# Ten of the 22 contraction tiles of the down projection as five pairs of seven half-block products

## The chip, the cores and the metric

One NeuronCore of a Trainium2 chip runs the whole program, and it is alone on the chip. The metric is the device time of one execution in microseconds (us). Lower is better. The kernel is written by hand, engine by engine: each engine has its own list of instructions, and semaphores are the only thing that orders one list against another. The engines are TensorE (PE; its weight loads are listed as PEld), VectorE (DVE), ScalarE (ACT), GpSimd (POOL) and SyncE (SP), which issues the DMAs.

## The reference

Two layers (DEPTH 2) run over x of 512 positions by 1024 channels, in float32. Each layer is a mixer (gMLP gating and differential attention) and a SwiGLU; the change is in the last product of the SwiGLU:

```python
for l in range(DEPTH):
    ...
    h = rms_norm(x, pre_ffn_g[l])
    gu = jnp.einsum('bsd,df->bsf', h, w_gate_up[l])
    gate, up = gu[..., :FFN_HIDDEN], gu[..., FFN_HIDDEN:]
    y = jnp.einsum('bsf,fd->bsd', jax.nn.silu(gate) * up, w_down[l])
    x = x + rms_norm(y, post_ffn_g[l])
```

FFN_HIDDEN is 2816, that is 22 contraction tiles of 128 (`FT`).

## The kernel before

**Three passes.** Every float32 factor is kept as a high part (a copy rounded to fp32r) and a low part (the factor less its high part, again fp32r). `product` (L594 to L597) issues three matmuls for each pair of tiles: high by high, low by high, high by low. So each weight block is copied by ACT to `w_hi` (`high`, L1060) and subtracted by POOL to `w_lo` (`low`, L529, two pieces of 128x512).

**Weights.** Weights come in chunks c = 0 to NC-1. A chunk has two halves h, each of 128x1024 floats (512 KB). `raw` holds two chunks, `w_hi` and `w_lo` two chunks as well, looked at as eight slots of 128x512 where the gate and up projections need it. SP's `load_half` (L439) reads a half once the lows of the same half two chunks before are made; `high` waits for the data and for the slot's earlier user (`w_done`, which PE raises).

**Gate and up.** Tiles f = 0 and 1 are plain. From f = 2 (`F0`) on, one chunk per f is a 2x2 block matrix B (rows: halves of the contraction; columns: gate and up), and the left factor is 2x2 as well (halves of the positions by halves of the contraction). They are multiplied with seven block products instead of eight (`gate_up_blocks`, L789), in the form with sums S1 to S4 of the left factor and T1 to T4 of B. DVE makes the T sums (`t_sum`, L1771), POOL five of seven lows, DVE two. T1 and T2 lie in PSUM banks, so that most of DVE's instructions there have one operand in PSUM.

**Down.** The hidden matrix (high `hid_hi`, low `hid_lo`, 128 x 22 x 512 each: contraction tile by positions) is the stationary factor, the weights stream as 512 columns. Eleven chunks of four tiles, first all 22 tiles of the left 512 output columns, then of the right ones. For each half chunk (two tiles) PE runs four rows of 128 positions, 6 matmuls each (`down_part`, L816), into banks 0 to 3 (left) and 4 to 7 (right). The last two chunks go row by row (`down_rows`, L825), so that the rows of the result end one after the other. Both `turn_rows` calls of the next group's first two rows (transposes of the normalised x) stand in the midst of rows 2 and 3.

```python
for c in range(C_DOWN, LAST - 1):
    for h in range(2):
        half, k = divmod(4 * (c - C_DOWN) + 2 * h, FT)
        rows = (2, 3, 0, 1) if k == 0 and half == 0 else (0, 1, 2, 3)
        for r in rows:
            ...
            down_part(l, c, h, r, rows[-1])
```

**Before the first down chunks.** SP has loaded the first two down chunks while the gate and up projections ran. When their last product is done, it issues four reads of 512 KB of x from the spill buffer, `gpost`, in layer 0 `gpre` (each of 1024 values for 128 partitions), and only then the third down chunk (L504 to L511).

**The boundary.** For each row of positions: ACT squares the right half (`root_of_branch`, L1108), DVE multiplies by the gain and adds to x (`residual`, L1534), ACT takes the root of the new row, DVE normalises it (`norm_row`, L1497), PE turns it. After layer 1 the same is done without the next norm, and the row is stored.

## Time and profile before

| | |
|---|---|
| median of 3 runs | 1084.99 us (1084.96 to 1085.32) |
| profiled execution | 1084.86 us |
| its span, first to last instruction | 1082.7 us |
| PE busy | 1074.8 us, 99% of the span |
| PEld, DVE, ACT, POOL busy | 89%, 56%, 54%, 52% |
| granted TensorE clock, mean | 0.999 |
| HBM traffic over the span | 109 GB/s |

The profiled execution is 2.2 us longer than its span; the rest lies ahead of the first instruction and behind the last one. Busy shares are of the span; a line number is that of the kernel before. Matmuls overlap in the records: the time from one start to the next, not the duration, is what one costs.

### The profile page before, as it was taken

How to read it: one execution, taken by the hardware profiler on the slowest of the kernel's cores; microseconds unless marked ns; L12 is line 12 of the kernel's file. 1: busy time of each engine (PE TensorE's matmuls, PEld its weight loads, DVE VectorE, ACT ScalarE, POOL GpSimd, SP SyncE). 2: the span in 40 equal slices, each digit the busy share in tenths (PEclk: the TensorE clock that was granted, in tenths of full speed). 3: DMA queues.
4: the chain of work that ended last, by engine and by line, in shares of the span. 5: the costliest groups of instructions: out<-in, count | busy, mean ns of one | idle time of the engine just before them, and what ended most of it. 6: DMA issues, size and time to landing. Idle time of an engine off the chain costs nothing.

```text
span 1082.7 us, 17501 instructions
## 1 busy us (share of the span) xinstructions
PE 1074.8 (99%) x6788; PEld 965.0 (89%) x6788; DVE 608.6 (56%) x1011; ACT 589.5 (54%) x1151; POOL 568.1 (52%) x442
## 2 busy tenths in 40 slices
PE   9999999999999999999999999999999999999997
PEld 7888788999999999888888888889999999988886
DVE  4376554878888884010344756457888888820103
ACT  6767784755555554221457568656655555531212
POOL 3534364467666665544344344634766666654440
PEclk9999999999999999999999999999999999999999
DMA  8423212424433434523353222232343343363212
GB/s 291 147 60 104 71 59 81 153 79 118 117 100 97 118 103 169 176 97 97 87 161 103 78 79 78 75 126 87 103 117 100 96 117 107 91 218 119 98 51 78
DMA packets 145335, 119.37 MB, mean 110 GB/s; under 512 B 3802, under 2 KB 120036, under 8 KB 145252
## 3 DMA queue, kind: packets, MB, share of 16 engines
q1 hardware_dynamic: 145236, 118.24, 35.1%
q8 instruction: 54, 0.88, 0.3%
q14 instruction: 29, 0.24, 0.1%
q10 hardware_dynamic: 16, 0.00, 0.0%
HBM read 111.94 MB, written 6.29 MB: 109 GB/s over the span
## 4 chain that ended last, share of the span: by engine, by line
PE 99%; ACT 0%; DMA 0%; DVE 0%; issue 0%; DVEq 0%; ACTq 0%
PE banks L595 30%; PE banks L597 30%; PE banks L596 30%; PE banks L660 2%; PE banks L688 2%; PE banks L604 1%; PE banks L673 1%; PE banks L865 1%; PE banks L699 1%; DMA x_rows<-in_x_dram 0%; PE banks L706 0%; ACT junk L1080 0%; PE banks L950 0%; DVE scratch L1509 0%; DVE x_rows L1543 0%
## 5 line engine op out<-in xcount | busy, mean ns | idle before, releaser
L534 POOL TENSOR_TENSOR w_lo<-raw,w_hi 128x512 fp32r<-128x512 f32 x204 | 264.7, 1321 | 312.2 <-ACT w_hi L1072 312.2
L552 POOL TENSOR_TENSOR w_lo<-raw,w_hi 128x512 fp32r<-128x512 f32 x200 | 260.8, 1314 | 146.6 <-ACT w_hi L1141 142.1
L595 PE MATMUL banks<-xg_hi,w_hi 128*128 128x256 f32 (+1 forms) x880 | 273.5, 311 | 0.0
L597 PE MATMUL banks<-xg_lo,w_hi 128*128 128x256 f32 (+1 forms) x880 | 271.3, 308 | 0.0
L596 PE MATMUL banks<-xg_hi,w_lo 128*128 128x256 f32 (+1 forms) x880 | 271.2, 308 | 0.0
L1072 ACT ACTIVATE w_hi<-raw 128x1024 fp32r<-128x1024 f32 x102 | 107.2, 1061 | 161.4 <-PE banks L597 146.9
L1141 ACT ACTIVATE w_hi<-raw 128x512 fp32r<-128x512 f32 x200 | 125.1, 630 | 114.9 <-DVE raw L1794 61.1
L597 PEld LDWEIGHTS banks<-xg_lo,w_hi 128*128 128x128 f32 x880 | 168.0, 191 | 8.4
L595 PEld LDWEIGHTS banks<-xg_hi,w_hi 128*128 128x128 f32 x880 | 168.1, 191 | 8.3
L596 PEld LDWEIGHTS banks<-xg_hi,w_lo 128*128 128x128 f32 x880 | 168.1, 191 | 7.5
L595 PE MATMUL banks<-w_hi,hid_hi 128*128 128x512 f32 x352 | 137.2, 390 | 0.0
L597 PE MATMUL banks<-w_lo,hid_hi 128*128 128x512 f32 x352 | 137.0, 389 | 0.0
L596 PE MATMUL banks<-w_hi,hid_lo 128*128 128x512 f32 x352 | 137.0, 389 | 0.0
L595 PE MATMUL banks<-s_part,w_hi 128*128 128x256 f32 x480 | 135.8, 283 | 0.0
L596 PE MATMUL banks<-s_part,w_lo 128*128 128x256 f32 x480 | 135.8, 283 | 0.0
L597 PE MATMUL banks<-s_part,w_hi 128*128 128x256 f32 x480 | 135.8, 283 | 0.0
L595 PEld LDWEIGHTS banks<-s_part,w_hi 128*128 128x128 f32 x480 | 92.2, 192 | 0.0
L596 PEld LDWEIGHTS banks<-s_part,w_lo 128*128 128x128 f32 x480 | 92.2, 192 | 0.0
L597 PEld LDWEIGHTS banks<-s_part,w_hi 128*128 128x128 f32 x480 | 92.2, 192 | 0.0
L1800 DVE TENSOR_TENSOR w_lo<-banks,w_hi 128x512 fp32r<-128x512 f32 x80 | 54.8, 686 | 51.8 <-ACT w_hi L1141 51.8
L1531 DVE TENSOR_TENSOR banks<-banks,gpost 128x512 f32<-128x512 f32 x16 | 10.6, 696 | 126.6 <-ACT junk L1106 126.6
L597 PEld LDWEIGHTS banks<-w_lo,hid_hi 128*128 128x128 f32 x352 | 66.1, 188 | 13.8
(180 smaller groups left out, 1875.8 us busy)
## 6 DMA issues: line engine op xcount, KB each, us to landing
raw<-in_w_gate_up_dram SPq DMA_DIRECT2D x88, 512.0 KB, 4.1
raw<-in_w_down_dram SPq DMA_DIRECT2D x44, 512.0 KB, 3.8
raw<-in_w_in_dram SPq DMA_DIRECT2D x40, 512.0 KB, 3.8
raw<-in_w_out_dram SPq DMA_DIRECT2D x16, 512.0 KB, 3.7
x_spill<-x_rows SPq DMA_DIRECT2D x8, 512.0 KB, 4.3
x_rows<-x_spill SPq DMA_DIRECT2D x8, 512.0 KB, 4.9
x_rows<-in_x_dram SPq DMA_DIRECT2D x4, 512.0 KB, 7.4
out_dram<-x_rows SPq DMA_DIRECT2D x8, 256.0 KB, 2.1
```

Of the source, the lines that this page charges most:

```text
L534: last = tt(lo[:, piece], raw_half(l, c, h)[:, piece], hi[:, piece].bitcast(F32), ALU.subtract)
L552: tt(lo, full, hi.bitcast(F32), ALU.subtract).then_inc(w_ready, 1)
L595: mm(o, stat[0], mov[0], start=first, stop=False)
L596: mm(o, stat[1], mov[0], start=False, stop=False)
L597: return mm(o, stat[0], mov[1], start=False, stop=last)
L604: last = tr(b_tr[turned_bank(group, r, half)][:, k, :], xn[:, r % 2, at:at + P], ident[:, :])
L660: last = mm(bank[SC_BANKS[n % 2][j]][:, 0:w], q[ps, h, i * P:(i + 1) * P], k[ps, h, 0:w], start=(n_pass == 0), stop=(n_pass == 2))
L673: last = tr(b_tr[T_BANK][:, at + k, :], attn[n % 2][:, k * P:(k + 1) * P], ident[:, :])
L688: last = mm(bank[O_BANK][:, (n % 2) * P:(n % 2 + 1) * P], attn_t(n, k), v_att[:, k, h * P:(h + 1) * P], start=(k == 0), stop=(k == i))
L1072: fn(high_low(l, c, h)[0], raw_half(l, c, h), ACT.Copy).then_inc(w_hi_ready, 1)
L1141: fn(factor(l, f, i)[0], full, ACT.Copy).then_inc(w_hi_ready, 1)
L1800: tt(lo, t_place(l, f, i), hi.bitcast(F32), ALU.subtract).then_inc(t_ready, 1)
```

## The change

The down projection takes tiles 0 to 9 as five pairs. In each pair the 2x2 left factor A has the first and the second tile of the pair as columns and positions 0 to 255 and 256 to 511 as rows; B has the two tiles as rows and the left and right 512 output columns as columns. Seven products stand for eight:

- chunk P (one per pair): A11 by B11 into banks 4 and 5, A12 by B21 into banks 0 and 1, S3 by T3 into 6 and 7, A22 by T4 into 2 and 3; each 2 row blocks by 3 passes, 24 matmuls for the chunk
- chunk Q (one per pair, read from HBM once more without B21): S4 by B22 into 4 and 5, S1 by T1 into 6 and 7, S2 by T2 into 0 and 1; 18 matmuls
- tiles 10 to 21 stay plain, 48 matmuls a chunk: `("L", 10)`, `("L", 14)`, `("L", 18)`, called left 10, left 14 and left 18 here, and right 10, right 14, right 18.

Over the five pairs the products accumulate in the banks, and DVE puts the results together afterwards: `add_p7`, `add_left`, `add_p6_left`, `add_p5`, `add_p6`. The left half of y now lies in SBUF (`y_left_of`). In the boundary each row of the right half gets one more addition on DVE ahead of ACT's square. Through the gate and up projections, copies and lows of f = 0 to 9 are cut in two or get a further addition.

All sums of the weights are DVE instructions with both inputs in `raw` or `w_hi`, in SBUF; `pair_sums` makes three for P and two for Q, `pair_lows` two for each. `h_sums` and `h_low` are four and four instructions of 128x1280, both inputs in SBUF.

```diff
     C_VG, C_QK, C_VA, C_QK2, C_U, C_OUT, C_GU = 0, 2, 4, 6, 8, 10, 14
     C_DOWN = C_GU + FT
-    NC = C_DOWN + 2 * FT // 4
+    NP = 5
+    K0_PLAIN = 2 * NP
+    DOWN = [("L", 10), ("P", 0), ("P", 1), ("L", 14), ("P", 2), ("P", 3), ("P", 4), ("L", 18),
+            ("Q", 0), ("Q", 1), ("Q", 2), ("Q", 3), ("Q", 4), ("R", 10), ("R", 14), ("R", 18)]
+    NC = C_DOWN + len(DOWN)
...
+    C_P, C_Q = [[C_DOWN + DOWN.index((kind, p)) for p in range(NP)] for kind in "PQ"]
+    C_L_END, C_R0 = C_DOWN + DOWN.index(("L", 18)), C_DOWN + DOWN.index(("R", 10))
+    P_B11, P_B21, P_T3, P_T4 = range(4)
+    Q_B22, Q_T1, Q_T2 = range(3)
...
+        H_PARTS = {"A11": (hid_hi[:, first_of_pair, left], hid_lo[:, first_of_pair, left]),
+                   "A12": (hid_hi[:, second_of_pair, left], hid_lo[:, second_of_pair, left]),
+                   "A22": (hid_hi[:, second_of_pair, right], hid_lo[:, second_of_pair, right]),
+                   "S3": (part_hi[:, 0:NP, :], hid_lo[:, first_of_pair, right]),
+                   "S1": (part_hi[:, NP:2 * NP, :], hid_hi[:, first_of_pair, right]),
+                   "S2": (part_hi[:, 2 * NP:3 * NP, :], part_lo[:, 0:NP, :]),
+                   "S4": (part_lo[:, NP:2 * NP, :], part_lo[:, 2 * NP:3 * NP, :])}
+        H_FULL = {"S3": hid_full[:, 1, first_of_pair, right], "S1": hid_full[:, 0, first_of_pair, right],
+                  "S2": part_full[:, 1, 0:NP, :], "S4": part_full[:, 1, 2 * NP:3 * NP, :]}
+        H_SUMS = ("S3", "S1", "S2", "S4")
...
+        def y_left_of(r):
+            return hid_full[:, r // 2, 4 + 2 * (r % 2):6 + 2 * (r % 2), left]
...
-                    sp.wait_ge(w_ready, low_upto(m, d, LOW_OF[B22 if h else T4] if blocks(d) else h))
+                    if kind_of(d) == "P":
+                        if h == 0:
+                            sp.wait_ge(w_ready, low_upto(m, d, P_B21))
+                            sp.wait_ge(pair_added, pair_added_upto(m, d, 2))
+                        else:
+                            sp.wait_ge(pair_ready, pair_upto(m, d, 1))
+                    elif kind_of(d) == "Q":
+                        if h == 1:
+                            sp.wait_ge(w_ready, low_upto(m, d, Q_B22))
+                        sp.wait_ge(pair_ready, pair_upto(m, d, 1))
+                    else:
...
+            def pair_low(l, c, i):
+                hi, lo = factor_of(l, c, i)
+                pool.wait_ge(w_hi_ready, upto(l, c, i))
+                tt(lo, pair_raw(l, c, i), hi.bitcast(F32), ALU.subtract).then_inc(w_ready, 1)
...
+                start = K0_PLAIN if kind == "L" or r >= 2 else None
+                last = wide_part(l, c, h, o, hid_left(r), range(k, k + 2), start, FT - 1)
                 if r == last_row:
                     last.then_inc(w_done, 1)
                 elif k + 2 == FT:
-                    last.then_inc(y_b_done if half else y_a_done, 1)
+                    last.then_inc(y_b_done if kind == "R" else y_a_done, 1)
...
+            def pair_product(l, c, i, part, o, first, last):
+                p = DOWN[c - C_DOWN][1]
+                hi, lo = factor_of(l, c, i)
+                for j in range(2):
+                    at = slice(j * P, (j + 1) * P)
+                    done = product(bank[o + j][:, :], (H_PARTS[part][0][:, p, at], H_PARTS[part][1][:, p, at]), (hi, lo),
+                                   first and p == 0, last and p == NP - 1)
+                done.then_inc(w_done, 1)
...
+            def left_pair(l, p):
+                c = C_P[p]
+                if p == 0:
+                    pe.wait_ge(hid_ready, FT * (l + 1))
+                pe.wait_ge(w_ready, low_upto(l, c, P_B11))
+                pair_product(l, c, P_B11, "A11", 4, True, True)
+                pe.wait_ge(w_ready, low_upto(l, c, P_B21))
+                pair_product(l, c, P_B21, "A12", 0, False, False)
+                pe.wait_ge(pair_ready, pair_upto(l, c, 0))
+                if p == 0:
+                    pe.wait_ge(h_ready, 4 * l + 1)
+                pair_product(l, c, P_T3, "S3", 6, True, True)
+                pe.wait_ge(pair_ready, pair_upto(l, c, 1))
+                pair_product(l, c, P_T4, "A22", 2, False, False)
...
+            def right_pair(l, p):
+                c = C_Q[p]
+                pe.wait_ge(w_ready, low_upto(l, c, Q_B22))
+                if p == 0:
+                    pe.wait_ge(h_ready, 4 * (l + 1))
+                    pe.wait_ge(p1_kept, 2 * (l + 1))
+                pair_product(l, c, Q_B22, "S4", 4, True, False)
+                pe.wait_ge(pair_ready, pair_upto(l, c, 0))
+                if p == 0:
+                    pe.wait_ge(p7_added, 2 * (l + 1))
+                pair_product(l, c, Q_T1, "S1", 6, True, True)
+                pe.wait_ge(pair_ready, pair_upto(l, c, 1))
+                if p == 0:
+                    pe.wait_ge(y_left_added, 4 * l + 2)
+                pair_product(l, c, Q_T2, "S2", 0, True, True)
...
                     gate_up_blocks(l, f)
                 for c in range(C_DOWN, LAST - 1):
-                    for h in range(2):
-                        half, k = divmod(4 * (c - C_DOWN) + 2 * h, FT)
-                        rows = (2, 3, 0, 1) if k == 0 and half == 0 else (0, 1, 2, 3)
-                        for r in rows:
-                            if c == C_DOWN and h == 0 and r < 2:
...
-                        act.wait_ge(w_done, upto(l - 1, C_DOWN + 6, 0))
+                        act.wait_ge(w_done, upto(l - 1, C_Q[1], Q_T1))
...
+                def pair_high(c, i):
+                    kind, p = DOWN[c - C_DOWN]
+                    if (kind, i) in (("P", P_B11), ("P", P_B21), ("Q", Q_B22)):
+                        n = NC * l + c
+                        act.wait_ge(raw_landed[n % 2][kind == "Q"], 16 * (n // 2 + 1))
+                    else:
+                        act.wait_ge(pair_added, pair_added_upto(l, c, {P_T3: 0, P_T4: 2}[i] if kind == "P" else i - 1))
+                    if ring[l, c, i][1] is not None:
+                        act.wait_ge(w_done, ring[l, c, i][1])
+                    fn(factor_of(l, c, i)[0], pair_raw(l, c, i), ACT.Copy).then_inc(w_hi_ready, 1)
...
+                    act.wait_ge(w_done, upto(l, C_P[NP - 1], P_B11))
+                    fn(silu_t[:, j, :], bank[4 + j][:, :], ACT.Copy).then_inc(p1_kept, 1)
...
                 silu_21(FT - 1)
                 hidden_high(FT - 1)
+                h_high("S3")
                 for c in range(C_DOWN + 1, NC):
-                    both_high(l, c)
-                    if c == C_DOWN + 6:
+                    if paired(c):
+                        for i in range(DONE_OF[kind_of(c)]):
+                            pair_high(c, i)
+                    else:
+                        both_high(l, c)
+                    if c == C_P[3]:
+                        for name in H_SUMS[1:]:
+                            h_high(name)
+                    elif c == C_L_END:
...
+                y_b = y_right_of(b, r)
+                if b % 2:
+                    if r < ST - 1:
+                        dve.wait_ge(y_b_done, 3 * b + r + 1)
+                    else:
+                        dve.wait_ge(w_done, upto(b // 2, LAST, 1))
+                    dve.wait_ge(p6_added, ST * (b // 2) + r + 1)
+                    tt(y_b, y_b, silu_t[:, r, :], ALU.add).then_inc(y_b_added, 1)
                 dve.wait_ge(ssq_b_ready, ST * b + r + 1)
...
+                def h_sums():
+                    a11, a12 = [[t.bitcast(F32) for t in H_PARTS[name]] for name in ("A11", "A12")]
+                    s1, s2, s4 = [H_FULL[name] for name in ("S1", "S2", "S4")]
+                    tt(s2, s1, a11[0], ALU.subtract).then_inc(h_added, 1)
+                    dve.wait_ge(h_added, 4 * l + 1)
+                    tt(s2, s2, a11[1], ALU.subtract).then_inc(h_added, 1)
+                    dve.wait_ge(h_added, 4 * l + 2)
+                    tt(s4, a12[0], s2, ALU.subtract).then_inc(h_added, 1)
+                    dve.wait_ge(h_added, 4 * l + 3)
+                    tt(s4, s4, a12[1], ALU.add).then_inc(h_added, 1)
...
+                def pair_sums(c):
+                    n = NC * l + c
+                    for h in range(2):
+                        dve.wait_ge(raw_landed[n % 2][h], 16 * (n // 2 + 1))
+                    b11, b12, b22 = [raw_half(l, c, col)[:, row * SE:(row + 1) * SE] for row, col in ((0, 0), (0, 1), (1, 1))]
+                    if kind_of(c) == "P":
+                        b21 = raw_half(l, c, 0)[:, SE:2 * SE]
+                        tt(b12, b22, b12, ALU.subtract).then_inc(pair_added, 1)
+                        dve.wait_ge(pair_added, pair_added_upto(l, c, 0))
+                        tt(b22, b12, b11, ALU.add).then_inc(pair_added, 1)
+                        dve.wait_ge(pair_added, pair_added_upto(l, c, 1))
+                        tt(b22, b21, b22, ALU.subtract).then_inc(pair_added, 1)
+                    else:
+                        tt(b12, b12, b11, ALU.subtract).then_inc(pair_added, 1)
+                        dve.wait_ge(pair_added, pair_added_upto(l, c, 0))
+                        tt(b11, b22, b12, ALU.subtract).then_inc(pair_added, 1)
...
+                def pair_lows(c):
+                    for i in (P_T3, P_T4) if kind_of(c) == "P" else (Q_T1, Q_T2):
+                        hi, lo = factor_of(l, c, i)
+                        dve.wait_ge(w_hi_ready, upto(l, c, i))
+                        tt(lo, pair_raw(l, c, i), hi.bitcast(F32), ALU.subtract).then_inc(pair_ready, 1)
...
+                def add_p6_left(j):
+                    y = y_left_of(2 + j)
+                    if j == 0:
+                        dve.wait_ge(w_done, upto(l, C_Q[NP - 1], Q_T2))
+                    dve.wait_ge(y_left_added, 4 * (l + 1))
+                    tt(y, y, in_two(bank[j][:, :]), ALU.add).then_inc(y_left_ready, 1)
...
+                    pair_lows(C_P[p])
+                    if p == 1:
+                        h_sums()
+                for name in H_SUMS[1:]:
+                    h_low(name)
+                add_p7(0)
+                add_p7(1)
+                pair_sums(C_Q[0])
+                pair_lows(C_Q[0])
+                pair_sums(C_Q[1])
+                for r in range(ST):
+                    add_left(r)
+                pair_lows(C_Q[1])
+                for p in range(2, NP):
+                    pair_sums(C_Q[p])
+                    pair_lows(C_Q[p])
+                add_p6_left(0)
+                add_p6_left(1)
+                for r in range(ST):
+                    add_p5(r)
+                for r in range(ST):
+                    add_p6(r)
                 if l < L - 1:
```

**DVE, from the last low of the hidden matrix in layer 0.** Before, the gains of the boundary follow at once:

```order
L1834 TENSOR_TENSOR banks<-banks,silu_t 128x512
L1838 TENSOR_TENSOR hid_lo<-banks,hid_hi 128x512
L1531 TENSOR_TENSOR banks<-banks,gpost 128x512 x4
L1532 TENSOR_SCALAR bias_a<-ssq_a 128x4
L1536 TENSOR_TENSOR banks<-banks,gpost 128x512
```

Now the low of S3, the sums and lows of P0 and P1, and the four sums of the hidden matrix come first (what is in brackets are the semaphores waited for):

```order
L2074 TENSOR_TENSOR hid_lo<-banks,hid_hi 128x512 [waits hid_hi_ready]
L2080 TENSOR_TENSOR hid_lo<-hid_full,xg_hi 128x5x256 [waits h_hi_ready]
L2102 TENSOR_TENSOR raw<-raw 128x512 [waits raw_landed11,raw_landed10]
L2104 TENSOR_TENSOR raw<-raw 128x512 [waits pair_added]
L2106 TENSOR_TENSOR raw<-raw 128x512 [waits pair_added]
L2117 TENSOR_TENSOR w_lo<-raw,w_hi 128x512 [waits w_hi_ready] x2
L2102 TENSOR_TENSOR raw<-raw 128x512 [waits raw_landed01,raw_landed00]
L2104 TENSOR_TENSOR raw<-raw 128x512 [waits pair_added]
L2106 TENSOR_TENSOR raw<-raw 128x512 [waits pair_added]
L2117 TENSOR_TENSOR w_lo<-raw,w_hi 128x512 [waits w_hi_ready] x2
L2086 TENSOR_TENSOR part_full<-hid_full,hid_hi 128x1280
L2088 TENSOR_TENSOR part_full<-part_full,hid_lo 128x1280 [waits h_added]
```

DVE had nothing between those places; now it makes 69 instructions per layer there before the gains.

**ACT, at the same place of the new program**, the high parts of P0, P1 and left 14:

```order
L1594 ACTIVATE hid_hi<-banks 128x512 [waits prod_done]
L1615 ACTIVATE xg_hi<-hid_full 128x1280 [waits w_done,hid_ready]
L1606 ACTIVATE w_hi<-raw 128x512 [waits w_done,raw_landed10] x2
L1606 ACTIVATE w_hi<-raw 128x512 [waits w_done,pair_added] x2
L1606 ACTIVATE w_hi<-raw 128x512 [waits w_done,raw_landed00] x2
L1606 ACTIVATE w_hi<-raw 128x512 [waits w_done,pair_added] x2
L1227 ACTIVATE w_hi<-raw 128x1024 [waits w_done,raw_landed10]
```

Before, a row `L1072 ACTIVATE w_hi<-raw 128x1024` stood for each half chunk, and none waited for DVE. Now the copies of left 14 (the last row) stand behind those of P1's sums.

## Rows read from the trace of the kernel before

**Rows 1.** The page: busy time, and the granted TensorE clock in 40 slices
```profile
PE 1074.8 (99%) x6788; PEld 965.0 (89%) x6788; DVE 608.6 (56%) x1011; ACT 589.5 (54%) x1151; POOL 568.1 (52%) x442
PEclk9999999999999999999999999999999999999999
```
**Rows 2.** The page: the chain that ended last, by engine
```profile
PE 99%; ACT 0%; DMA 0%; DVE 0%; issue 0%; DVEq 0%; ACTq 0%
```
**Rows 3.** Windows over the down projection of layer 0, then of layer 1
```profile
423.30:544.70 121.40, 121.40 (x546) 100.57 (x546) 17.50 (x32) 36.48 (x55) 56.16 (x44) 1.00 0.39 130
957.40:1077.20 119.80, 119.80 (x530) 98.85 (x528) 12.15 (x22) 28.83 (x40) 50.60 (x40) 1.00 0.33 114
```
**Rows 4.** Timeline of PE: start, us, line; its first down matmul
```profile
423.35 0.40 PE L595 MATMUL banks<-w_hi,hid_hi 128*128 128x512 f32 x1
```
**Rows 5.** Groups by line and form: DVE, POOL, ACT instructions that the change repeats
```profile
L1785 DVE TENSOR_TENSOR raw<-raw 128x512 f32<-128x512 f32 x40 | 31.1, 777 | 0.1
L1838 DVE TENSOR_TENSOR hid_lo<-banks,hid_hi 128x512 fp32r<-128x512 f32 x44 | 30.4, 690 | 9.7 <-ACT hid_hi L1422 7.3
L1822 DVE TENSOR_TENSOR banks<-banks,silu_t 128x256 f32<-128x256 f32 x40 | 17.3, 432 | 1.3
L534 POOL TENSOR_TENSOR w_lo<-raw,w_hi 128x512 fp32r<-128x512 f32 x41 | 51.9, 1289 | 51.5 <-ACT w_hi L1072 51.5
L1141 ACT ACTIVATE w_hi<-raw 128x512 fp32r<-128x512 f32 x200 | 125.1, 630 | 114.9 <-DVE raw L1794 61.1 <-PE banks L597 52.4 <-DVE raw L1785 1.2
```
**Rows 6.** One line's instructions (min/median/max ns): two SBUF inputs, DVE
```profile
L1785 DVE TENSOR_TENSOR raw<-raw x40: 675/677/1668, 214.5 to 940.6; 128x512 f32<-128x512 f32 x40
L1782 DVE TENSOR_TENSOR banks<-raw x40: 700/1614/1795, 213.8 to 938.5; 128x512 f32<-128x512 f32 x40
```
**Rows 7.** Timeline of DVE and POOL at 76 us
```profile
76.98 1.66 DVE L1634 SCALAR_TENSOR_TENSOR v_gate<-v_gate,ln_rs,ln_rows 128x512 f32<-128x512 f32 x1
78.57 1.78 DVE L1632 SCALAR_TENSOR_TENSOR v_gate<-v_gate,mv,ln_rows 128x512 f32<-128x512 f32 x1
80.39 1.66 DVE L1634 SCALAR_TENSOR_TENSOR v_gate<-v_gate,ln_rs,ln_rows 128x512 f32<-128x512 f32 x1
88.73 0.75 DVE L1634 SCALAR_TENSOR_TENSOR v_gate<-v_gate,ln_rs,ln_rows 128x512 f32<-128x512 f32 x1
...
76.61 6.57 POOL L534 TENSOR_TENSOR w_lo<-raw,w_hi 128x512 fp32r<-128x512 f32 x4 [11.98 <-ACT w_hi L1072]
```
**Rows 8.** Timeline of SP, then ACT, as the down projection of layer 0 starts
```profile
426.35 0.97 SPq L446 DMA_DIRECT2D raw<-in_w_down_dram  x2
...
426.42 2.00 ACT L1072 ACTIVATE w_hi<-raw 128x1024 fp32r<-128x1024 f32 x2
435.81 1.06 ACT L1072 ACTIVATE w_hi<-raw 128x1024 fp32r<-128x1024 f32 x1 [7.38 <-DMA raw<-in_w_down_dram]
437.12 1.06 ACT L1072 ACTIVATE w_hi<-raw 128x1024 fp32r<-128x1024 f32 x1 [0.25 <-DMA raw<-in_w_down_dram]
```
**Rows 9.** Timeline of ACT, the same place in layer 1
```profile
970.38 1.06 ACT L1072 ACTIVATE w_hi<-raw 128x1024 fp32r<-128x1024 f32 x1 [0.35 <-DMA raw<-in_w_down_dram]
```
**Rows 10.** Timeline of DVE, then PE and POOL, at the boundary of the layers
```profile
532.77 1.41 DVE L1509 SCALAR_TENSOR_TENSOR scratch<-x_rows,rs_x,gpre 128x512 f32<-128x512 f32 x2
534.97 0.70 DVE L1536 TENSOR_TENSOR banks<-banks,gpost 128x512 f32<-128x512 f32 x1 [0.79 <-ACT junk L1115]
538.92 1.42 DVE L1509 SCALAR_TENSOR_TENSOR scratch<-x_rows,rs_x,gpre 128x512 f32<-128x512 f32 x2
...
534.93 1.03 PE L604 MATMUL banks<-ident,scratch 128*128 128x128 f32 x8
541.26 1.04 PE L604 MATMUL banks<-ident,scratch 128*128 128x128 f32 x8
...
533.49 5.58 POOL L534 TENSOR_TENSOR hid_lo<-raw,hid_hi 128x512 fp32r<-128x512 f32 x4 [8.27 <-ACT hid_hi L1072]
```
**Rows 11.** Timeline of ACT, then DVE, behind the last matmul
```profile
1077.34 0.60 ACT L1115 ACTIVATE junk<-banks 128x512 bf16<-128x512 f32 x1 [4.42 <-PE banks L597]
1078.06 0.70 DVE L1536 TENSOR_TENSOR banks<-banks,gpost 128x512 f32<-128x512 f32 x1 [3.23 <-ACT junk L1115]
```

232 lines of the change are left out of this document (183 added, 49 removed).

## The prediction

> **What bounds the kernel now.** I read the page first: the busy line shows PE busy for 1074.8 of 1082.7 us at a full clock [rows 1]. A busy PE proves little by itself, so the chain comes next: 99% of it is PE, and no other engine has 1% [rows 2]. So every matmul taken out is worth its slot, as long as what feeds PE keeps up. The windows over the two down projections give the slot: 119.8 us for the 528 matmuls of layer 1 (the row counts two more, which reach in from the neighbours), 0.227 us each; layer 0 takes 121.4 us with 16 small transposes of the next norm among them [rows 3]. In the same rows DVE is busy 17 and 12 us and POOL 56 and 51: there is room beside PE, and this change fills it.
>
> **What it removes.** Per pair 24 + 18 = 42 matmuls stand for 48: per layer 5 x 6 = 30, in all 60. All have 512 columns as before, and the stationary side stays 128 x 128, so each is worth 0.227 us: 60 x 0.227 = **-13.6 us**. The sum goes by order, with the time of a P chunk 24 x 0.227 = 5.44 us, of a Q chunk 4.08, of a plain one 10.9.
>
> **What it adds beside PE.** Per layer: DVE makes 25 sums and 20 lows of 128x512 with both inputs in SBUF, 0.68 us each [rows 5], together 30.6 us; and 8 instructions of 128x1280. Nothing in the trace is that wide; between 0.432 us at 256 and 0.690 at 512 columns an element costs 1.0 ns [rows 5], so I estimate 1.47 us each, 11.8 us. The 16 that read a PSUM bank come to 11 us. POOL loses lows: P takes 2, Q 1 of 128x512 at 1.29 us, a plain chunk 4. ACT copies 35 blocks at 0.63 us [rows 5], four wide ones and two banks in place of ten half chunks at 1.06 [rows 8], some 17 us more; with 36 and 29 us busy of 120 [rows 3] it has the room. DMA: a P chunk is 1 MB in 5.44 us, Q 0.75 MB in 4.08 us; raw buffers are freed by the sums and lows, so reads start late when DVE is late.
>
> **The port.** DVE with two SBUF inputs and POOL don't run side by side. L1785 takes 0.677 us in the median, when POOL is mostly idle, and up to 1.668; L1782, issued while POOL works, has a median of 1.614 [rows 6]. At 76 us three DVE instructions with SBUF inputs take 1.66, 1.78 and 1.66 us against 0.75 alone, and POOL's four take 6.57 us against 4 x 1.29 = 5.2 [rows 5, 7]. They take turns. From one start to the next that is 1.59 and 1.82 us for a DVE and a POOL instruction together [rows 7], while 0.75 + 1.29 would be 2.04. So a turn costs less than the sum of both, by about 0.2 us where both queue: I take 0.1 us back at each handover. The Trainium skill (SBUF — State Buffer, "SBUF: two separate sides") calls the pair of ports an exclusive lock held for the whole instruction, the other engine fully blocked. That DVE and POOL exclude each other the trace confirms; that nothing is saved at the handover it doesn't, by 1.6 to 1.8 against 2.04.
>
> How full does that make the port? From the last low of the hidden matrix (about 427.3 us) to the start of right 10 (423.35 [rows 4] + 354 matmuls x 0.227 = 503.7) there are 76 us. DVE brings 30.6 + 11.8 = 42.4, POOL 25 lows x 1.29 = 32.3: 74.7 if nothing overlapped, some 68 with handovers. It nearly fits, but the work can't be spread freely, since each step waits for slots, reads and the other engine.
>
> **Where it doesn't fit.** I followed the lists chunk by chunk with these durations. P0: hidden ready 427.3, S3's high 428.6, low 430.1, sums by about 434, all before PE needs T3 at 436.9. P1 was the third chunk in SP's list before, and is so now: its right half lands at 437.1, behind the four reads of x and the gains [rows 8]. Its three sums, alternating with POOL's two lows of P1, end at 440.7; T4's copy on ACT at 441.4; only then ACT takes left 14's first half (1.06 [rows 8]), done 442.4. POOL's two lows of it would take 2.6, but DVE is now in its four wide sums of 1.47 and they alternate: 447.0. PE has finished P1 at 445.1. So it **waits 2 us** there. In layer 1 the read lands at 970.38 - 957.4 = 13.0 us after the start against 13.8 [rows 3, 9]; a wait of 1.5 us. Behind it the chain has air: P4's and left 18's lows come 0.5 to 2 us ahead of PE, Q1 to Q4 2 to 5 us ahead, right 10 about level. **+3.5 us** for both layers. From below these waits could be zero (the port costs nothing); from above, without the saving at the handover, the same walk gives 5.1 and 4.5 us, 9.6 in all, with left 18 and right 10 late too; and each 0.5 us more on a read of a chunk adds 1.5 us a layer.
>
> **The boundary.** The first row's normalised x is ready at 532.77 + 1.41 = 534.2, PE's transposes start at 534.93: 0.75 us of air. The second at 540.3 against 541.26: 0.9 [rows 10]. The new addition of 0.70 us heads each row's chain, and for row 1 it also waits for DVE to finish row 0, ahead of ACT's square: 1.5 us late instead of 0.7. Besides, the left half of y is now in SBUF, so `residual`'s first step has two SBUF inputs and meets POOL's four lows of the next layer (533.49 to 539.1 [rows 10]), up to 0.9 us more. Row 0 comes just in time, row 1 about 1.3 us late, and its low for the next layer's first product once more about 1.2. **+2.5 us**, bounds 0.5 and 4.
>
> **The tail.** Behind the last matmul ACT squares the row, then DVE follows [rows 11]. One addition is put ahead, nothing hides it: **+0.8 us** (0.70 and a handover).
>
> **Gate and up.** For f = 0 to 9 DVE gets 2 x 0.43 in place of 0.69 on even tiles and 0.43 more on odd ones, ACT about 0.2 more. PSUM operands, so no port. The cover is DVE's idle fifth of a 10.1 us chunk; zero, and if it were gone, 10 x 0.4 = at most 4 us in both layers.
>
> **Sum.** Against the profiled execution of 1084.86: -13.6 + 3.5 + 2.5 + 0.8 + 0 = **1078.1 us**. The median of the runs lies 0.13 above it, so 1078.2.
>
> **Rivals.**
> - *The cover holds everywhere.* PE never waits for a factor; only boundary and tail cost. 1084.9 - 13.6 + 0.8 + 1 = 1073.1. For it: the work fits into 76 us. Against it: the order at left 14. 0.15.
> - *The port locks in full.* As for the forecast, with waits of 9.6: 1084.9 - 13.6 + 9.6 + 2.5 + 0.8 = 1084.2. The Trainium skill's rule (same page and section) would make the time this one. The pitch in rows 7 speaks against it; in its favour, dependent DVE instructions leave a gap in which POOL gets in each time. 0.15.
> - *Slower: the port becomes the bound.* DVE's and POOL's work in the stretch is 74.7 us of 76. If wide or strided operands in SBUF take 20% longer than I take (8.5 us more), the port and not PE sets the pace from left 14 to right 10: the walk then gives 10.7 us of waits a layer, and 1084.9 - 13.6 + 21.4 + 3.3 = 1096. It decides from 8 us of waits a layer; below that the kernel is no slower. For it: the total; against it: L1785's 0.68 with raw blocks of the very same shape. 0.10.
> - *The change doesn't do what it says.* The new order of PE has 60 matmuls fewer, so this is left with nearly nothing, and goes into the last case.
>
> The forecast's case has 0.60. About 0.2% (2.2 us) is what a measurement of this kernel can tell from no change. Faster by more than that (below 1082.8): 0.60 + 0.15 and a third of the second rival, 0.80. Within it: the rest of that rival, 0.09. Slower: 0.11. Range: from the first rival's 1073 to just above the second's, 1085.
>
> **What would show it.** The windows of the down projections would have 498 matmuls of 0.227 us, 113 us, plus the waits. PE's weight loads would wait for POOL's `w_lo` near 445 us, by some 2 us, and hardly anywhere else before the boundary; DVE's sums on `raw` would show a median well above 0.68 us, and POOL's lows some of 1.8. At the boundary the second pair of transposes would wait for DVE. The last DVE instruction would end 0.8 us further behind the last matmul than before. The forecast is wrong if PE waits more than 5 us in one down projection, if waits appear at the Q chunks (reads or slots late), if gate and up grow, or if the granted clock falls below its 0.999.

## The result, and the profile after

| | before | changed kernel |
|---|---|---|
| median (range, runs) | 1085.08 us (1084.96 to 1085.32, 4) | 1079.32 us (1077.71 to 1080.38, 4) |
| ratio | | 0.9945, 95% interval 0.9928 to 0.9963 |
| profiled execution, its span | 1084.86, 1082.7 us | 1078.91, 1076.9 us |
| granted TensorE clock, mean | 0.999 | 0.997 |

The changed kernel is 0.55% faster. 1078.2 us had been forecast, with 1073.0 to 1085.0 as the range.

The page of the changed kernel: the busy line, the row of the granted clock in its 40 slices, the chain by engine, and POOL's largest group, the lows of the weights. They answer to [rows 1, 2, 5].

```profile
PE 1064.0 (99%) x6728; PEld 954.5 (89%) x6728; DVE 765.0 (71%) x1177; ACT 621.1 (58%) x1223; POOL 585.2 (54%) x432
...
PEclk9999999999999999999999999999999999999999
...
PE 94%; DVE 2%; ACT 1%; DMA 1%; POOL 1%; issue 0%; SPq 0%; DVEq 0%; ACTq 0%
...
L627 POOL TENSOR_TENSOR w_lo<-raw,w_hi 128x512 fp32r<-128x512 f32 x164 | 233.9, 1452 | 226.9 <-ACT w_hi L1227 226.9
```

PE's share of the chain fell from 99% to 94%: at some places PE now waits for what the others prepare. DVE rose from 56% to 71% of the span. A low on POOL takes 1.45 us on average. The row of the clock shows no loss, since each of its slices is 27 us long; the mean of 0.997 is its only sign on the page.

The windows of the changed kernel: the down projection of layer 0, then the same stretch in three pieces (4.45 us in the middle stand apart), then layer 1. Columns: us, busy (x count) of PE, PEld, DVE, ACT, POOL, granted clock, DMA share, GB/s. The first and last row answer to [rows 3].

```profile
423.30:542.20 118.90, 116.73 (x516) 96.09 (x515) 91.02 (x100) 50.95 (x82) 64.52 (x39) 0.99 0.50 166
423.30:447.40 24.10, 21.98 (x98) 17.88 (x96) 19.34 (x19) 10.03 (x15) 11.49 (x7) 1.00 0.76 262
447.45:451.90 4.45, 4.45 (x12) 3.51 (x13) 4.42 (x3) 0.00 (x0) 4.45 (x2) 0.62 0.35 118
451.90:542.20 90.30, 90.30 (x407) 74.70 (x406) 67.22 (x80) 40.91 (x67) 48.53 (x32) 1.00 0.44 143
955.90:1070.60 114.70, 113.34 (x500) 93.19 (x498) 88.18 (x94) 44.83 (x71) 58.38 (x35) 1.00 0.45 154
```

Two losses show. In layer 0 PE is idle for over 2 us ahead of 447.45. And the 4.45 us behind that hold only 12 matmuls, with PE busy throughout and a granted clock of 0.62, while the rows above and below stand at 1.00. In layer 1 the clock stays at 1.00.

PE's timeline in the changed kernel at that place: start us, us, engine, line; in brackets the idle time before it and who ended it.

```profile
447.45 0.50 PE L699 MATMUL banks<-w_hi,hid_hi 128*128 128x512 f32 x1 [2.17 <-POOL w_lo L627]
447.79 0.40 PE L700 MATMUL banks<-w_hi,hid_lo 128*128 128x512 f32 x1
448.02 0.47 PE L701 MATMUL banks<-w_lo,hid_hi 128*128 128x512 f32 x1
448.29 0.63 PE L699 MATMUL banks<-w_hi,hid_hi 128*128 128x512 f32 x1
448.71 0.63 PE L700 MATMUL banks<-w_hi,hid_lo 128*128 128x512 f32 x1
...
451.27 0.56 PE L700 MATMUL banks<-w_hi,hid_lo 128*128 128x512 f32 x1
451.67 0.40 PE L701 MATMUL banks<-w_lo,hid_hi 128*128 128x512 f32 x1
451.90 0.40 PE L699 MATMUL banks<-w_hi,hid_hi 128*128 128x512 f32 x1
```

This is the first product of left 14. The matmul ahead of it began at 444.89, so the wait is 447.45 - 444.89 - 0.227 = 2.33 us (below, every "wait" is this distance of two starts less a matmul's 0.227 us). From 448.29 on the starts are 0.42 to 0.43 us apart instead of 0.227: 512 columns at 1.2 GHz, the lower of TensorE's two levels, in place of 2.4 GHz. Seven distances are like that, 0.2 us lost in each, and four others are longer by 0.04 to 0.17 us. From 447.45 to 451.90 that makes 4.45 us for 12 distances, 4.45 - 12 x 0.227 = **1.73 us** lost in all; then the clock is back. Some 0.11 us of it, the first distance behind the wait, is lost behind the waits without a fall of the clock too.

Who held left 14's factors back: the timeline of DVE, then of POOL, of the changed kernel.

```profile
442.29 1.49 DVE L2086 TENSOR_TENSOR part_full<-hid_full,hid_hi 128x1280 f32<-128x1280 f32 x1
443.81 2.47 DVE L2088 TENSOR_TENSOR part_full<-part_full,hid_lo 128x1280 f32<-128x1280 f32 x1
446.31 2.43 DVE L2090 TENSOR_TENSOR part_full<-hid_hi,part_full 128x1280 f32<-128x1280 f32 x1
448.78 2.45 DVE L2092 TENSOR_TENSOR part_full<-part_full,hid_lo 128x1280 f32<-128x1280 f32 x1
...
442.68 9.70 POOL L627 TENSOR_TENSOR w_lo<-raw,w_hi 128x512 fp32r<-128x512 f32 x4 [2.97 <-ACT w_hi L1227]
```

One wide sum alone takes 1.49 us, the other three 2.43 to 2.47. POOL's four lows of left 14 take 9.70 us, 2.43 each, where the same instruction took 1.29 before [rows 5]. So DVE and POOL alternate, as the prediction had drawn it for just this place.

The waits of PE's weight loads, by what ended them (us in total, times, longest):

```profile
PEld banks L699 <- POOL w_lo L627: 5.4, 7, 2.6
PEld banks L708 <- DVE scratch L1714: 1.3, 1, 1.3
...
PEld banks L699 <- DVE xg_lo L1726: 1.0, 1, 1.0
```

Two of the seven waits for POOL reach PE: 2.33 us at 447.45, 1.52 us at 979.24 in layer 1. The one for `scratch` is at the start of the program (the row of L1714 starts at 6.2 us) and was there before. The one for `xg_lo` is new: 0.74 us at 544.41, inside the first product of the next layer, where its second row of positions begins.

**Where the time went.** The spans of the two profiled executions, cut at the same matmuls:

| stretch | before | after | difference |
|---|---|---|---|
| to the first down matmul of layer 0 | 423.35 | 423.33 | -0.02 |
| down 0, up to the next layer's first matmul | 121.55 | 118.98 | -2.57 |
| from there to the first down matmul of layer 1 | 412.51 | 413.62 | +1.11 |
| down 1, up to its last matmul's start | 119.50 | 114.41 | -5.09 |
| from there to the end of the span | 5.82 | 6.56 | +0.74 |

Down 0: -6.8 for 30 matmuls, + 2.33 waited, + 1.73 behind the wait, leaves 0.17 open. Down 1: -6.8 + 1.52, leaves 0.2 open, 0.11 of it the first distance behind the wait.

### The profile page after: what moved, and what is told of

The parts are those of the page before. It is cut to its first block, busy times and chain, and to the rows that moved or that the text cites. A ratio compares the mean times of both kernels' runs of the same rounds, so it can differ in the third digit from the quotient of the medians.

```text
span 1076.9 us, 17751 instructions
## 1 busy us (share of the span) xinstructions
PE 1064.0 (99%) x6728; PEld 954.5 (89%) x6728; DVE 765.0 (71%) x1177; ACT 621.1 (58%) x1223; POOL 585.2 (54%) x432
## 4 chain that ended last, share of the span: by engine, by line
PE 94%; DVE 2%; ACT 1%; DMA 1%; POOL 1%; issue 0%; SPq 0%; DVEq 0%; ACTq 0%
PE banks L699 29%; PE banks L701 29%; PE banks L700 29%; PE banks L764 2%; PE banks L792 2%; PE banks L708 1%; PE banks L777 1%; PE banks L1015 1%; POOL w_lo L627 1%; DMA raw<-in_w_down_dram 1%; PE banks L803 1%; ACT junk L1235 0%; DMA x_rows<-in_x_dram 0%; PE banks L810 0%; DVE x_rows L1766 0%
## 5 line engine op out<-in xcount | busy, mean ns | idle before, releaser
L627 POOL TENSOR_TENSOR w_lo<-raw,w_hi 128x512 fp32r<-128x512 f32 x164 | 233.9, 1452 | 226.9 <-ACT w_hi L1227 226.9
L645 POOL TENSOR_TENSOR w_lo<-raw,w_hi 128x512 fp32r<-128x512 f32 x200 | 261.3, 1317 | 146.1 <-ACT w_hi L1308 141.6
L1308 ACT ACTIVATE w_hi<-raw 128x512 fp32r<-128x512 f32 x200 | 124.9, 631 | 115.4 <-DVE raw L2020 61.2
L1227 ACT ACTIVATE w_hi<-raw 128x1024 fp32r<-128x1024 f32 x82 | 86.0, 1061 | 42.8 <-PE banks L701 36.8
L700 PE MATMUL banks<-w_hi,hid_lo 128*128 128x512 f32 x272 | 106.5, 392 | 0.0
L699 PE MATMUL banks<-w_hi,hid_hi 128*128 128x512 f32 x252 | 99.3, 394 | 3.5 <-POOL w_lo L627 3.5
L701 PE MATMUL banks<-w_lo,hid_hi 128*128 128x512 f32 x252 | 98.7, 392 | 0.0
L1606 ACT ACTIVATE w_hi<-raw 128x512 fp32r<-128x512 f32 x70 | 42.3, 628 | 81.3 <-DVE raw L2102 23.3
L699 PE MATMUL banks<-w_hi,xg_hi 128*128 128x512 f32 x220 | 87.1, 396 | 0.0
```

The costliest lines, as they stand in the source:

```text
L627: last = tt(lo[:, piece], raw_half(l, c, h)[:, piece], hi[:, piece].bitcast(F32), ALU.subtract)
L645: tt(lo, full, hi.bitcast(F32), ALU.subtract).then_inc(w_ready, 1)
L699: mm(o, stat[0], mov[0], start=first, stop=False)
L700: mm(o, stat[1], mov[0], start=False, stop=False)
L701: return mm(o, stat[0], mov[1], start=False, stop=last)
L1227: fn(high_low(l, c, h)[0], raw_half(l, c, h), ACT.Copy).then_inc(w_hi_ready, 1)
```

## The experiments

"Before" in each table cell is the kernel before, run on the same chip in turn with the others.

### a0: the changed kernel once more

The spread of 2.7 us over four executions, against 0.4 for the kernel before, was itself in need of a cause.

> The changed kernel once more, beside the others, since its four times so far spread over 2.7 us. Theory A (POOL's lows of left 14 alternate with DVE's wide sums; PE waits 2.3 us in layer 0 and 1.5 in layer 1; a clock drop behind the longer wait costs another 1.7): 1077.5 to 1080.5, with the drop of the granted clock in some executions and not in others. Rival B (the wait is that of a late read, the spread comes from elsewhere): the same wait each time, no link between a wait and the clock.

1078.97 us (1078.03 to 1080.89, 5 runs) against 1085.07 (9 runs): 0.9946 [0.9932, 0.9959]. In this profile the waits at left 14 are 2.80 us in layer 0 and 1.08 in layer 1. Its window behind the longer one (columns as above):

```profile
448.00:453.00 5.00, 4.92 (x15) 3.90 (x16) 4.96 (x3) 0.00 (x0) 5.00 (x4) 0.66 0.30 105
```

15 matmuls in 5 us, where 22 fit: the same fall of the clock, at the same place. It belongs to the kernel, not to one execution.

### e1: without the four wide sums

```diff
                     pair_sums(C_P[p])
                     pair_lows(C_P[p])
-                    if p == 1:
-                        h_sums()
```

`S2` and `S4` are then read from what lies in their place, so that ACT and PE have the work they had. ACT's wait for the sums goes with them.

> Leaves out the four wide sums of the hidden matrix (S2 and S4 are made from what lies in their place). Theory A: left 14's four lows take 5.2 us in a row instead of 9.7, PE's wait before left 14 falls from 2.3 and 1.5 us to 0 or 0.2, the clock stays full, and 5.5 us are gained against the changed kernel: 1073 to 1074.5. Rival B (P1's read, landing behind the reads of x, or ACT's order is what ends last): a wait of 1.5 us or more stays before left 14 and at most 2 us are gained.

1073.47 us (1073.26 to 1074.11, 4 runs): 0.9894 [0.9880, 0.9907]. POOL's lows of left 14, then the waits of PE's weight loads for POOL:

```profile
442.69 5.04 POOL L627 TENSOR_TENSOR w_lo<-raw,w_hi 128x512 fp32r<-128x512 f32 x4 [2.97 <-ACT w_hi L1227]
...
PEld banks L699 <- POOL w_lo L627: 2.2, 7, 0.7
```

The lows start at the same moment (442.69 against 442.68) and take 5.04 us instead of 9.70. PE's wait falls under 0.25 us in layer 0 and to 0.46 in layer 1; the clock stays up. The four sums a layer cost 5.9 us (from 1079.32) or 5.5 (from a0's 1078.97), though DVE has the time for them: it is where they stand that costs.

### e2: the wide sums spread

The same work in other places: one sum behind P1's lows, one behind P2's, two behind P3's, where nothing needs them before Q1's chunk.

```diff
-                    if p == 1:
-                        h_sums()
+                    for n in {1: (0,), 2: (1,), 3: (2, 3)}.get(p, ()):
+                        h_sum(n)
```

> Same work, the four wide sums spread over DVE's list: one behind P1, one behind P2, two behind P3. Theory A: left 14's lows meet one of them instead of three, the wait falls to 0.3 to 1 us, the clock stays full, other waits of up to 1 us may appear before P4 and left 18; 1074 to 1076. Rival B: no change against the changed kernel beyond 1 us. A third possibility, that the port is simply full: the wait moves to P4, left 18 or Q0 with its 2 us and more, 1077 to 1080.

1075.51 us (1074.73 to 1076.02, 4 runs): 0.9911 [0.9897, 0.9924]. The wait at left 14 is 1.19 us in layer 0, a little more than expected, and 0.20 in layer 1. A new one of 0.17 stands ahead of right 10. There is no slow matmul. Of 3.85 us of waits 2.3 are gone, and with them the 1.73: 4.0 us by this sum, 3.6 by the spans of the two profiles, 3.8 by the medians.

### e3: without the new addition

The other part of the change, at the boundary and the end: the right half of y has its P6 part added before ACT squares it. Here it isn't added.

```diff
-                    dve.wait_ge(p6_added, ST * (b // 2) + r + 1)
-                    tt(y_b, y_b, silu_t[:, r, :], ALU.add).then_inc(y_b_added, 1)
```

> Leaves out the addition on DVE ahead of ACT's square in each row's chain of the boundary and of the end (the right half then lacks the products kept in silu_t in rows). Everything else as in the changed kernel. My sum has 2.5 us for the boundary and 0.8 for the tail, the trace shows some 1.3 and 0.77: expected is a gain of 0.7 to 0.8 behind the last matmul and of 0.8 to 1.3 in front of the next layer, 1.6 to 2.1 in all, 1077.3 from 1079.3. Rival: the boundary's loss comes from the left half that now lies in SBUF and meets POOL's lows; then only the 0.8 of the tail and less than 0.4 at the boundary come back.

1077.09 us (1075.28 to 1077.76, 5 runs): 0.9924 [0.9911, 0.9936]. From the next layer's first matmul to down 1 it takes 412.5 us again (412.51 before, 413.62 after), and from the last matmul to the end 5.84 (5.82 and 6.56). So the addition costs 1.1 us at the boundary and 0.7 at the end. The waits at left 14, 2.78 and 1.85 us, and the slow matmuls are still there: the two parts are independent.

### e4, e5, e10: a wait put into the kernel before

Is it the wait that brings the clock down, or the change's other work? The kernel before has no wait and nothing of the change. PE is made to wait in each layer ahead of the third down chunk for one wide DVE instruction, issued when the second chunk is done. e4 has 2048 elements a partition, e5 1024 and e10 3072.

```diff
+                        if c == C_DOWN + 2 and h == 0:
+                            pe.wait_ge(gap_done, l + 1)
...
+                dve.wait_ge(w_done, upto(l, C_DOWN + 1, 1))
+                tt(xg_hi[:, 0:4, :].rearrange("p k s -> p (k s)"),
+                   hid_hi[:, 0:4, :].bitcast(F32).rearrange("p f s -> p (f s)"),
+                   hid_lo[:, 0:4, :].bitcast(F32).rearrange("p f s -> p (f s)"), ALU.add).then_inc(gap_done, 1)
```

> The kernel before, with one added DVE instruction of 128x2048 per layer that starts when PE has finished the second down chunk and that PE must wait for ahead of the third: a wait of 2.4 us in each layer and nothing else. Theory A (a wait of that length makes the granted clock fall for a while, whatever caused it): besides the 2 x 2.4 us of waiting, matmuls behind it start 0.43 us apart for some 9 of them, 1.75 us more a layer: 1085.0 + 4.8 + 3.5 = 1093.3. Rival: the drop in the changed kernel had another cause (load on the other engines, chance): 1089.8, full clock.

> As e4_gap_two with a DVE instruction of 128x1024: a wait of 1.3 us in each layer. Theory A, by the changed kernel's layer 1 (a wait of 1.5 us, no drop): 1085.0 + 2.6 = 1087.6 and a full clock. Rival (any wait of PE over 1 us lowers the clock): 1091.

> As e4_gap_two with 128x3072: a wait of about 3.7 us in each layer of the kernel before. e4_gap_two had a wait of 2.61 in each layer and the full clock in its profile, 5.2 us of the 5.3 to 5.4 that its two quickest executions lost; two of four were 1.2 and 3.1 us above those. Theory A (a longer wait lowers the clock more often): most executions above 1085.1 + 7.4 + 1.7 = 1094.2, and a stretch of matmuls 0.43 us apart in the profile. Rival (chance, or the load of the other engines in the changed kernel): as e4_gap_two, quickest executions at 1092.5 and full clock.

| | waits in the profile | 1085.08 + waits | measured | slow distances in the profile |
|---|---|---|---|---|
| e5 | 2 x 1.55 us | 1088.2 | 1088.30 (1088.02 to 1088.39, 7) | none |
| e4 | 2 x 2.61 us | 1090.3 | 1090.39, 1090.50, 1091.66, 1093.56 | none |
| e10 | 2 x 3.68 us | 1092.4 | 1093.94, 1095.64, 1096.96, 1097.22 | 13 and 7 |

The ratios to before: 1.0029 [1.0018, 1.0040], 1.0062 [1.0046, 1.0079], 1.0100 [1.0085, 1.0115]. First e4's window behind its wait, its profile being that of the 1090.50:

```profile
450.00:455.00 5.00, 5.00 (x24) 4.13 (x22) 0.00 (x0) 1.06 (x1) 0.37 (x2) 1.00 0.33 105
```

Then e10's: two of layer 0, one of layer 1.

```profile
450.00:455.00 5.00, 5.00 (x13) 3.93 (x12) 0.00 (x0) 0.00 (x0) 1.27 (x2) 0.50 0.32 105
455.00:460.00 5.00, 5.00 (x23) 4.05 (x23) 0.00 (x0) 1.06 (x1) 1.18 (x1) 0.98 0.00 0
990.00:995.00 5.00, 5.00 (x16) 3.95 (x16) 0.00 (x0) 0.00 (x0) 2.09 (x2) 0.66 0.32 104
```

A wait alone is enough: behind 3.68 us of idle PE the granted clock is 0.50, 13 matmuls stand where 22 would, and DVE does nothing there. In that profile 3.0 us are lost behind the wait of layer 0 and 1.7 behind that of layer 1; with the waits that gives 1097.1, and 1097.22 was measured. Waits of 1.55 us cost themselves and little more.

At 2.61 us it goes either way: two executions lie on the sum, two 1.2 and 3.1 us above it, and the one that was profiled has the full clock. The mean granted clock of each execution says the same: 0.999 for the two on the sum, 0.997 and 0.996 for the two above it. In the profiles of the changed kernel 2.33 and 2.80 us brought the clock down, in e3's 2.78. What decides between the two at such a length is open. Length alone doesn't, since 2.33 brought it down and 2.61 didn't. In all four profiles with a fall in layer 0 (the changed kernel, a0, e3, e10) the granted clock is 0.50 from 448.2 to 448.5 us on, in the changed kernel only 0.75 us after PE has resumed. Where a wait lies in time may thus count as well; no run moves a wait of one length, so this is not shown.

The Trainium skill (TensorE: Matmul & The Clock Gate, "Why this matters for your kernels") also puts such drops down to idle gaps of PE, and e10 agrees. The same page ("Wait — 56ns, not 53.3ns?") gives 426.7 ns as the distance of two starts at 512 columns in the lower state; the trace agrees, with 0.42 to 0.43 us.

### e7, e8: the port by itself

In the kernel before, 24 instructions of 128x512 on DVE are put beside POOL's ordinary lows, each waiting for the one before it. In e7 both inputs are in SBUF, in e8 one is in PSUM.

```diff
+                for n in range(24):
+                    tt(xg_hi[:, n % 3, :], hid_hi[:, 0, :].bitcast(F32),
+                       hid_lo[:, 1, :].bitcast(F32), ALU.add).then_inc(beside_done, 1)
+                    dve.wait_ge(beside_done, 24 * l + n + 1)
```

That is e7; in e8 `bank[4][:, :]` stands for the `hid_lo` block. PE waits for all 24 only ahead of the right half, long after they are done.

> The kernel before, in whose left half of the down projection DVE is idle, with 24 added DVE instructions of 128x512 per layer, both inputs in SBUF, one behind the other, beside POOL's lows. Theory A (the two engines take turns): where they meet, DVE's take about 1.67 us instead of 0.68 and POOL's pairs of lows 3.5 us and more instead of 2.54; PE isn't late, time within 1 us of the kernel before. Rival (the long DVE instructions of the changed kernel come from waits on semaphores or from DMA traffic into raw): 0.68 and 2.54 throughout.

> As e7_port_sbuf with the second input in a PSUM bank. Theory A: 0.69 us each for DVE and 2.54 for POOL's pairs, no meeting of the two. Rival (any DVE work beside POOL slows both): as long as in e7_port_sbuf.

1084.70 and 1084.85 us, one run each: as expected, no cost to PE. First e7, DVE and then POOL:

```profile
445.56 17.41 DVE L1896 TENSOR_TENSOR xg_hi<-hid_hi,hid_lo 128x512 fp32r<-128x512 f32 x16 [18.15 <-PE banks L598]
...
446.69 3.14 POOL L535 TENSOR_TENSOR w_lo<-raw,w_hi 128x512 fp32r<-128x512 f32 x2 [1.27 <-ACT w_hi L1075]
452.13 3.27 POOL L535 TENSOR_TENSOR w_lo<-raw,w_hi 128x512 fp32r<-128x512 f32 x2 [2.30 <-ACT w_hi L1075]
457.57 3.40 POOL L535 TENSOR_TENSOR w_lo<-raw,w_hi 128x512 fp32r<-128x512 f32 x2 [2.17 <-ACT w_hi L1075]
```

The same rows of e8:

```profile
445.71 17.30 DVE L1896 TENSOR_TENSOR xg_hi<-hid_hi,banks 128x512 fp32r<-128x512 f32 x24 [18.15 <-PE banks L598]
...
446.83 2.55 POOL L535 TENSOR_TENSOR w_lo<-raw,w_hi 128x512 fp32r<-128x512 f32 x2 [2.08 <-ACT w_hi L1075]
452.27 2.55 POOL L535 TENSOR_TENSOR w_lo<-raw,w_hi 128x512 fp32r<-128x512 f32 x2 [2.89 <-ACT w_hi L1075]
457.72 2.55 POOL L535 TENSOR_TENSOR w_lo<-raw,w_hi 128x512 fp32r<-128x512 f32 x2 [2.89 <-ACT w_hi L1075]
```

With an input in PSUM all 24 pass in 17.3 us, 0.72 each, and POOL's pairs keep their 2.55. With both in SBUF 16 take 17.41, that is 5.9 us more than 16 x 0.72, for six lows of POOL: each low, 1.28 us alone, costs DVE 0.98. POOL's pairs take 3.14 to 3.40 us, somewhat less than the 3.5 expected. So a DVE and a POOL instruction that meet take 0.3 us less than the sum of both, and the wide sums say the same: 2.47 from one to the next, against 1.49 + 1.29 = 2.78. The Trainium skill (SBUF — State Buffer, "SBUF: two separate sides") names, beside a 2-port mode of DVE, the DVE instructions with two SBUF inputs as those that contend with a GpSimd instruction that reads SBUF. These two runs agree.

### e6, e9: a version that beats both

e6 is e2 with the first wide sum behind P0, ahead of P1's read, where DVE has nothing to do. e9 is e6 with the next row's addition made at the boundary before this row's norm, so that it isn't in ACT's way when ACT's square comes.

```diff
-                    for n in {1: (0,), 2: (1,), 3: (2, 3)}.get(p, ()):
+                    for n in {0: (0,), 2: (1,), 3: (2, 3)}.get(p, ()):
```

```diff
-                if b % 2:
-                    ...
-                    tt(y_b, y_b, silu_t[:, r, :], ALU.add).then_inc(y_b_added, 1)
+                if b % 2 and (r == 0 or b == 2 * L - 1):
+                    add_right(b, r)
...
+                    if b % 2 and r < ST - 1:
+                        add_right(b, r + 1)
                     norm_row(group, r)
```

> As e2_spread (1075.5, one wait of 1.2 us left before left 14 in layer 0), with the first wide sum behind P0 instead of behind P1, so that none stands beside left 14's first lows. If those lows are what PE waits for: the wait falls below 0.5 us, 1074.3 to 1075.3. Rival: P1's three sums and two lows are pushed back by the 1.5 us of the wide sum, and left 14's copy on ACT with them; then the wait stays at 1.2 us or grows, 1075.5 to 1077.

> As e6_spread_earlier, and at the boundary of the layers the addition for row r + 1 stands ahead of row r's norm on DVE, in its idle time, instead of behind it. e3_no_addition gave back all of the 1.1 us in front of the next layer, so the addition's place in the list is the suspect: 0.5 to 1.1 us less than e6_spread_earlier, 1073.5 to 1074.5; the wait of 0.75 us before row 1 of the next layer's first product shrinks. Rival: ACT's square of row 1 waits for ACT's own copies of the next layer's weights, whatever DVE does; then under 0.4 us.

e6: 1074.45 us (1074.14 to 1074.66, 4 runs), 0.9903 [0.9886, 0.9919]; its waits at left 14 are 0.30 and 0.28 us. e9: **1073.72 us** (1073.45 to 1074.00, 4 runs), 0.9895 [0.9880, 0.9910]. The windows of e9's two down projections, then DVE's addition for row 1 at the boundary:

```profile
423.30:539.10 115.80, 115.61 (x518) 95.14 (x517) 90.61 (x103) 51.71 (x84) 61.32 (x40) 1.00 0.52 171
951.60:1066.00 114.40, 113.52 (x501) 93.22 (x499) 87.00 (x95) 44.90 (x72) 55.75 (x35) 1.00 0.45 154
...
532.97 0.70 DVE L1754 TENSOR_TENSOR banks<-banks,silu_t 128x512 f32<-128x512 f32 x1 [0.28 <-PE banks L701]
```

The same 60 matmuls fewer, the same DVE and POOL work, and layer 0's down projection takes 115.8 us instead of 118.9, at the full clock. The stretch behind it is back at 412.5 us: the boundary costs nothing. Left are waits of 0.31 and 0.20 us in layer 0 (left 14, right 10) and 0.30 in layer 1 (left 14), with about 0.1 behind each, and the addition at the end. e9 is 5.6 us faster than the changed kernel, about twice the gain for the same arithmetic.

## Why the prediction was right, point by point

Forecast for the profiled execution 1078.1 us, measured 1078.91. The forecast's own case is the one that happened. That the total came so close is in part luck: the sum hides two errors that nearly cancel, the clock (+1.73, no term for it) and the boundary (-1.4, too high).

- **What bounds it, and the slot of a matmul**: right. Down 1 has the 498 matmuls forecast, and with the waits shown it leaves 0.2 us open around -6.8, down 0 0.17.
- **The wait ahead of left 14**: place, holder (POOL's `w_lo`), cause (the wide sums at the port) and size right. Forecast 2 and 1.5 us, measured 2.33 and 1.52 (2.80 and 1.08 in a0). e1 takes the sums away and the wait goes; e2 and e6 move them and it shrinks to 1.19 and to 0.30. A wide sum, estimated at 1.47 us, takes 1.49 alone.
- **The saving at a handover**: taken at 0.1 us from a pair saving of 0.2; e7 gives 0.3 for a low. The rival *the port locks in full* rested on a saving of nothing and on waits of 9.6 us, where 3.85 were measured; it is out.
- **The Q chunks and the rest of the chain**: PE waited for nothing there, as forecast. *The port becomes the bound* is out: 3.85 us of waits in both layers, against 8 in each.
- **What was missing: the clock.** The walk priced a wait at its own length. In layer 0 the wait of 2.33 us was followed by 1.73 us lost to slow matmuls, three quarters of its own price again. The prediction named a granted clock below 0.999 only among its signs of being wrong, with no term and no case. This sign came, with 0.997. e10 shows that a wait alone does it.
- **The sign on DVE's sums**: forecast as a median well above 0.68 us. DVE's sums on `raw` blocks (min/median/max ns) in the changed kernel, answering to [rows 6]:

```profile
L2102 DVE TENSOR_TENSOR raw<-raw x10: 684/1771/1794, 430.0 to 995.0; 128x512 f32<-128x512 f32 x10
...
L2104 DVE TENSOR_TENSOR raw<-raw x10: 691/1668/1671, 431.8 to 995.7; 128x512 f32<-128x512 f32 x10
...
L2106 DVE TENSOR_TENSOR raw<-raw x10: 691/692/1666, 433.5 to 996.4; 128x512 f32<-128x512 f32 x10
```

  It holds for two of the three sums of a P chunk: their median is the contended time. The third mostly finds POOL idle. Of the two sums of a Q chunk one has 1.71 us in the median and the other 0.69. POOL's lows were to show some of 1.8 us, and several take 1.74 to 1.83; those beside the wide sums take 2.5.
- **The boundary**: mechanism right (the addition heads each row's chain, e3 shows it), size too high. Forecast +2.5, measured +1.1, 0.74 of it the wait at 544.41. The second pair of transposes, where a wait of 1.3 us had been expected, starts at 538.60 with no wait of PE before it. PE's rows, then DVE's rows of the changed kernel at the boundary, answering to [rows 10]:

```profile
538.60 1.11 PE L708 MATMUL banks<-ident,scratch 128*128 128x128 f32 x8
544.41 0.50 PE L699 MATMUL banks<-hid_hi,xg_hi 128*128 128x512 f32 x1 [0.59 <-DVE xg_lo L1726]
...
530.83 1.42 DVE L1718 SCALAR_TENSOR_TENSOR scratch<-x_rows,rs_x,gpre 128x512 f32<-128x512 f32 x2
532.16 0.69 DVE L1755 TENSOR_TENSOR banks<-banks,silu_t 128x512 f32<-128x512 f32 x1
533.60 0.70 DVE L1757 TENSOR_TENSOR banks<-banks,gpost 128x512 f32<-128x512 f32 x1 [0.75 <-ACT junk L1282]
534.40 0.77 DVE L1766 SCALAR_TENSOR_TENSOR x_rows<-hid_full,rs_y,x_rows 128x512 f32<-128x512 f32 x1
...
537.58 1.42 DVE L1718 SCALAR_TENSOR_TENSOR scratch<-x_rows,rs_x,gpre 128x512 f32<-128x512 f32 x2
538.91 0.69 DVE L1726 TENSOR_TENSOR xg_lo<-banks,xg_hi 128x512 fp32r<-128x512 f32 x1
```

  The addition follows the norm of row 0 at once, and the read of y in SBUF takes 0.77 us: the meeting with POOL's lows that was priced at up to 0.9 didn't happen. In e9's profile the same step takes 1.28 us, so it can. The step that failed is "row 1 about 1.3 us late". Before, row 1's norm ended at 540.34, 0.92 us ahead of the transposes; now it ends at 539.00, 0.4 us behind their start. It is thus 1.3 us later against PE than before, and 0.9 of that was air. PE starts on the first half of the row while DVE makes the second, so only 0.07 us are lost there. The low's lateness, forecast at 1.2 us, cost 0.74 and 0.11 behind it.
- **The tail**: forecast 0.8, measured 0.74. ACT's and DVE's rows there, answering to [rows 11]:

```profile
1070.77 0.70 DVE L1755 TENSOR_TENSOR banks<-banks,silu_t 128x512 f32<-128x512 f32 x1 [1.77 <-PE banks L701]
1071.50 0.60 ACT L1282 ACTIVATE junk<-banks 128x512 bf16<-128x512 f32 x1 [4.42 <-DVE banks L1755]
```

- **Gate and up at nothing**: right to 0.02 us, in layer 0 by the first row of the table, in layer 1 by e3's 412.5 us for the stretch that holds it.

By size: waits 0.35 us more, clock 1.73 more, boundary 1.4 less, some 0.3 not placed: the span fell by 5.8 us where 6.8 was forecast. The whole time fell by 5.95, 0.8 less than forecast.

The spread goes with the long waits. All executions of the kernel before, beside every experiment, lie within 0.6 us, e5's within 0.4, e6's 0.5, e9's 0.55, e1's 0.9, e2's 1.3; those with a wait of over 2 us spread by 2.7 (the changed kernel), 2.9 (a0), 2.5 (e3), 3.2 (e4) and 3.3 (e10). That the clock falls in some executions and not in others would give this. The mean granted clock of each execution bears it out in e4 (0.999 or 0.996 to 0.997), and e3's quickest, 1075.28, has 0.999 where its others have 0.997 or 0.998. It doesn't sort those of the changed kernel: the slowest and the quickest both have 0.998. So the clock is a part of the spread, and the rest is open.

Not tried: the right half's additions ahead of the last chunk, which would take the tail's 0.7 us as well.
